# Sixteen gate units split by accumulating transfers, and a norm's two sums moved in TensorE's order

## The reference

```
h = x @ w_in + b_in
conv_a, conv_g, q, k, v, r, f_lr, gate_a, gate_b = split(h)
y_conv = conv_module(conv_a, conv_g, ...)      # 31 taps, layer norm over channels, silu, @ w_conv_out
y_gla  = gla_branch(q, k, v, r, f_lr, ...)     # gated linear attention, 4 chunks of 64, @ w_gla_out
merged = sigmoid(gate_a) * y_conv + sigmoid(gate_b) * y_gla
x = layer_norm(alpha * x + merged @ w_out + b_out)
x = layer_norm(alpha * x + hier_moe(x))        # 64 experts, 8 groups, top 2
```

## Time and profile before

| what | value |
|---|---|
| median of three runs | 1691.71 us |
| the profiled execution | 1691.89 us, of which the span is 1689.8 us |
| PE busy | 1364.6 us (81%) |
| DVE busy | 674.2 us (40%) |
| ACT busy | 472.0 us (28%) |
| POOL busy | 59.0 us (3%) |
| chain that ended last | PE 51%, DMA 39%, DVE 6%, ACT 3% |
| DMA | 530.79 MB, 314 GB/s over the span, 432 GB/s from 400 to 1180 us |

### The profile page before, as it was taken

One profiled execution on the slowest core, in us unless ns is written; L12 is line 12 of the kernel. 1 busy time (PEld: TensorE's weight loads), 2 busy tenths in 40 slices (PEclk: granted clock), 3 DMA queues, 4 the chain that ended last, 5 costly groups with the idle time before them and its releaser, 6 DMA issues.

```text
span 1689.8 us, 21326 instructions
## 1 busy us (share of the span) xinstructions
PE 1364.6 (81%) x8600; PEld 883.5 (52%) x8600; DVE 674.2 (40%) x1109; ACT 472.0 (28%) x682; POOL 59.0 (3%) x27
## 2 busy tenths in 40 slices
PE   8999999976656666665666667566799999999998
PEld 7789988522212212221221222122499999778887
DVE  5787979311101100110111011001367888655874
ACT  4454233401001001010010010010265764546653
POOL 0000000670000000000000000000000000000000
PEclk9999999988787978887888888788999999999999
DMA  9433555899999999999999999999944325474440
GB/s 359 156 138 138 218 204 245 353 431 430 432 431 431 431 433 433 431 431 432 433 433 431 431 432 433 431 432 431 419 165 150 139 71 197 167 258 175 179 174 25
DMA packets 50441, 530.79 MB, mean 314 GB/s; under 512 B 4276, under 2 KB 5556, under 8 KB 33862
## 3 DMA queue, kind: packets, MB, share of 16 engines
q1 hardware_dynamic: 50374, 529.86, 75.8%
HBM read 528.80 MB, written 1.05 MB: 314 GB/s over the span
## 4 chain that ended last, share of the span: by engine, by line
PE 51%; DMA 39%; DVE 6%; ACT 3%; issue 1%; SPq 0%; DVEq 0%; ACTq 0%
DMA shared<-in_w 37%; PE psum L454 6%; PE psum L456 6%; PE psum L455 6%; PE psum L1433 6%; PE psum L367 5%; PE psum L2222 4%; PE psum L1456 4%; PE psum L2223 2%; PE psum L1462 2%; PE psum L1404 2%; PE psum L2059 1%; DVE ring_parts L590 1%; DMA arena<-in_w 1%; PE psum L611 1%
## 5 line engine op out<-in xcount | busy, mean ns | idle before, releaser
L1433 PE MATMUL psum<-ring,arena 128*32 128x512 f32 x992 | 145.3, 739 | 86.8 <-DMA ring<-in_w 86.6
L1433 PE MATMUL psum<-shared,arena 128*32 128x512 f32 x1040 | 151.0, 726 | 61.5 <-DMA shared<-in_w 61.4
L1665 DVE TENSOR_TENSOR shared<-shared,psum 128x512 f32<-128x512 f32 x16 | 11.0, 688 | 462.3 <-PE psum L1433 462.3
L1456 PE MATMUL psum<-shared 128*32 128x512 f32 x512 | 89.5, 834 | 68.4 <-DMA shared<-in_w 68.4
L454 PE MATMUL psum<-parts 128*128 128x256 f32 (+1 forms) x424 | 136.5, 322 | 0.7 <-DVE parts L532 0.7
L455 PE MATMUL psum<-parts 128*128 128x256 f32 (+1 forms) x424 | 135.1, 319 | 0.0
L1433 PEld LDWEIGHTS psum<-ring,arena 128*32 128x32 f32 x992 | 34.3, 132 | 185.3 <-DMA ring<-in_w 100.2
L456 PE MATMUL psum<-parts,ring_parts 128*128 128x256 f32 x464 | 131.2, 283 | 0.0
L1433 PEld LDWEIGHTS psum<-shared,arena 128*32 128x32 f32 x1040 | 38.2, 129 | 168.3 <-issue 91.8
L456 PE MATMUL psum<-parts 128*128 128x256 f32 (+1 forms) x392 | 126.1, 322 | 0.0
L454 PE MATMUL psum<-parts,ring_parts 128*128 128x256 f32 x400 | 114.8, 287 | 0.4 <-ACT shared L2256 0.4
(11 more groups left out here) (343 smaller groups left out, 2347.4 us busy)
## 6 DMA issues: line engine op xcount, KB each, us to landing
shared<-in_w SPq DMA_DIRECT2D x47, 4096.0 KB, 32.4
ring<-in_w SPq DMA_DIRECT2D x47, 4096.0 KB, 32.4
ring<-in_w_in SPq DMA_DIRECT2D x19, 2048.0 KB, 8.7
ring<-in_w_ffn_gate_up SPq DMA_DIRECT2D x11, 2048.0 KB, 8.2
ring<-in_w_gate SPq DMA_DIRECT2D x8, 2048.0 KB, 7.9
ring<-in_w_ffn_down SPq DMA_DIRECT2D x5, 2048.0 KB, 7.8
ring<-in_w_out SPq DMA_DIRECT2D x4, 2048.0 KB, 8.6
shared<-in_w SPq DMA_DIRECT2D x6, 1024.0 KB, 28.8
```

The source lines that it names most:

```text
L1433: m = pe.matmul(ps[slots, bank, :], V.picked[:, k, slots], w[e * len(w) // QUAD][:, e % (QUAD // len(w)), j, :], start=(k == 0), stop=(k = ...
L1456: m = pe.matmul(ps[slots, MOE_BANK["down"][c], :], V.hidden_t[:, f, slots], w(e), start=(f == 0), stop=(f == ET - 1))
```

## The change

1. InSplit goes on through gb0 and gb1: units 44 to 51 are multiplied in three passes as well.
2. For units 36 to 51 (ga0 to gb1) the low half is not made by DVE. ACT writes the negated rounded weight into the low buffer (a first activation with scale -1), then the high, and GpSimd issues a DMA that reads the unit's weights again from HBM (w_in_units, 512 KB each) and adds them to the low buffer. PE waits for the high and for the landing of that DMA.
3. These units have four buffers (A-slots 6, 12, 13, 14). Slot 6 holds v until then, so ACT's step 36 waits for the last product with v (kv3_1).
4. The ring places of ga and gb are free once ACT has made the highs, no longer with the lows or the matmuls.
5. moe_read0 is raised after gb1.
6. DVE's loop has no lows from step 36 on; its pace there is 7 taps (4 at steps 39 and 40, where it was 1).
7. conv_mean stands after two tiles of go0 and conv_var after four, before half and three quarters; DVE's and go's order follow (EndSplit's first two lows come after the normalization).
8. Some semaphores are shared between stages (piece_in, router_exp); the loads of ga and gb are laid out by unit in HBM.

```diff
-    SLABS = ["g0", "a1", "g1", "k", "v0", "v1", "q", "r0", "r1", "ga0", "ga1"]
+    SLABS = ["g0", "a1", "g1", "k", "v0", "v1", "q", "r0", "r1", "ga0", "ga1", "gb0", "gb1"]
-    BUFS = 3
+    BUFS, WIDE = 3, 4
+    BY_DMA = 4 * SLABS.index("ga0")
...
+        slot = 12 + n % self.BUFS if n < self.BY_DMA else (6, 12, 13, 14)[(n - self.BY_DMA) % self.WIDE]
...
     def high(self, L, n):
         src = self.source(L.eng, n)
-        if n >= self.BUFS:
-            self.wait_read(L.eng, n - self.BUFS)
+        if n == self.BY_DMA:
+            self.K.banks1.wait_full(L.eng, f"kv{NC - 1}_1")
+        elif n >= self.BUFS:
+            self.wait_read(L.eng, self.before(n))
+        if n >= self.BY_DMA:
+            L.done(L.eng.activation(self.part(n, 1), src, ACT.Copy, scale=-1.0), self.K.sem("in_minus"))
         L.done(L.eng.activation(self.part(n, 0), src, ACT.Copy), self.K.sem("in_high"))
+
+    def low_by_dma(self, pool, n):
+        m = n - self.BY_DMA
+        pool.wait_ge(self.K.sem("in_minus"), m + 1)
+        pool.dma_start(self.part(n, 1).rearrange("p k n -> p (k n)"), self.K.d["w_in_units"][m], accum_op=ALU.add)\
+            .then_inc(self.K.sem(f"low_added{m % self.WIDE}"), 16)
...
     def wait_low(self, eng, n):
-        eng.wait_ge(self.K.sem("in_low"), n + 1)
+        m = n - self.BY_DMA
+        if m < 0:
+            eng.wait_ge(self.K.sem("in_low"), n + 1)
+        else:
+            eng.wait_ge(self.K.sem("in_high"), n + 1)
+            eng.wait_ge(self.K.sem(f"low_added{m % self.WIDE}"), 16 * (m // self.WIDE + 1))
...
     slab_tiles("ga1", "ga", 4)
+    for s in range(2):
+        slab_tiles(f"gb{s}", "gb", 4 * s)
     pe.drain().then_inc(S("moe_read0"), FREED)
-    for s in range(2):
-        pe_slab_tiles(K, pe, B, R, f"gb{s}", tiles("gb", 4 * s, 4), x)
     pe.wait_ge(S("gla_conv"), GLA_CONV["gla_in"])
     y = K.tiles(7, DT)
-    pe_slab_tiles(K, pe, B, R, "go0", tiles("go", 0, 4), y)
+    pe_slab_tiles(K, pe, B, R, "go0", tiles("go", 0, 2), y, last=False)
     pe.wait_ge(S("gla_conv"), GLA_CONV["conv_sum"])
     pe_group(K, pe, B, "conv_mean", ...)
-    pe_slab_tiles(K, pe, B, R, "go1", tiles("go", 4, 2), y, last=False)
+    pe_slab_tiles(K, pe, B, R, "go0", tiles("go", 2, 2), y, first=2)
     pe.wait_ge(S("conv_squares"), 1)
     pe_group(K, pe, B, "conv_var", ...)
-    pe_slab_tiles(K, pe, B, R, "go1", tiles("go", 6, 2), y, first=2)
+    pe_slab_tiles(K, pe, B, R, "go1", tiles("go", 4, 4), y)
...
-    for n in range(split.units):
-        split.low(L, n)
+    for n in range(split.BY_DMA + 8):
+        if n < split.BY_DMA:
+            split.low(L, n)
         done = n - split.BUFS
-        pace = 0 if done < 0 else 2 if done < 4 or 8 <= done < 12 else 4
+        pace = 0 if done < 0 else 2 if done < 4 or 8 <= done < 12 else 4 if n < split.BY_DMA else 7
...
-            pace = 1
+            pace = 4
...
-    for m in range(4):
+    for m in range(2):
         gate_gla(m)
-    lows(0, 2)
...
-    for m in (4, 5):
+    for m in (2, 3):
         gate_gla(m)
...
-    gate_gla(6)
+    lows(0, 2)
     for m in range(DT):
+        if m % 2 == 0 and m < 6:
+            gate_gla(4 + m // 2)
         act_parts(m)
...
+def block1_pool(K, pool):
+    split = InSplit(K)
+    for n in range(split.BY_DMA, split.units):
+        split.low_by_dma(pool, n)
```

More of the change, by code:

```diff
@@ L348, in rstd, with first_slab_at @@
         return self.A(2, T, 1024 if i == 3 else 240 + T * i)
+    def first_slab_at(self, slot):
+        return self.ring_cols(slot * SLOT_COLS, SLOT_COLS).rearrange("p (m k n) -> p m k n", m=4, k=DT)
     def first_slab(self, ring):
-        return self.ring_cols(ring.slot("a0") * SLOT_COLS, SLOT_COLS).rearrange("p (m k n) -> p m k n", m=4, k=DT)
+        return self.first_slab_at(ring.slot("a0"))
     def slab(self, slot, k=DT):
@@ L503, in part, with before @@
         k = 2 if self.SLABS[n // 4] in self.ROWS else DT
-        return self.K.parts(12 + n % self.BUFS, 1024, 1024 * low).rearrange("p (k n) -> p k n", k=k)
+        slot = 12 + n % self.BUFS if n < self.BY_DMA else (6, 12, 13, 14)[(n - self.BY_DMA) % self.WIDE]
+        return self.K.parts(slot, 1024, 1024 * low).rearrange("p (k n) -> p k n", k=k)
+    def before(self, n):
+        if n == self.BY_DMA:
+            return None
+        return n - (self.WIDE if n > self.BY_DMA else self.BUFS)
     def source(self, eng, n):
         slab, i = self.SLABS[n // 4], n % 4
-        w = self.K.slab(self.K.ring1.wait_landed(eng, slab))
+        slot = self.K.ring1.wait_landed(eng, slab)
+        if n >= self.BY_DMA:
+            return self.K.first_slab_at(slot)[:, i]
+        w = self.K.slab(slot)
         return w[:, 2 * i:2 * i + 2, :] if slab in self.ROWS else w[:, :, i * P:(i + 1) * P]
@@ L524, in high @@
         src = self.source(L.eng, n)
-        if n >= self.BUFS:
-            self.wait_read(L.eng, n - self.BUFS)
-        L.done(L.eng.activation(self.part(n, 0), src, ACT.Copy), self.K.sem("in_high"))
+        if n == self.BY_DMA:
+            self.K.banks1.wait_full(L.eng, f"kv{NC - 1}_1")
+        elif n >= self.BUFS:
+            self.wait_read(L.eng, self.before(n))
+        if n >= self.BY_DMA:
+            L.done(L.eng.activation(self.part(n, 1), src, ACT.Copy, scale=-1.0), self.K.sem("in_minus"))
+        L.done(L.eng.activation(self.part(n, 0), src, ACT.Copy), self.K.sem("in_high"))
+    def low_by_dma(self, pool, n):
[3 more added lines that the diff above has]
+            .then_inc(self.K.sem(f"low_added{m % self.WIDE}"), 16)
     def low(self, L, n):
@@ L535, in wait_low @@
     def wait_low(self, eng, n):
-        eng.wait_ge(self.K.sem("in_low"), n + 1)
+        m = n - self.BY_DMA
[4 more added lines that the diff above has]
+            eng.wait_ge(self.K.sem(f"low_added{m % self.WIDE}"), 16 * (m // self.WIDE + 1))
 class EndSplit:
     UNITS, CONV = 16, 8
-    READ, FIRST = 3 * len(InSplit.ROWS), 4 * len(InSplit.SLABS)
+    READ, FIRST, FIRST_LOW = 3 * len(InSplit.ROWS), 4 * len(InSplit.SLABS), InSplit.BY_DMA
     def __init__(self, K):
@@ L605, in block1_pe @@
     for m in range(4):
-        pe.wait_ge(S(f"first_in{m}"), 16)
+        pe.wait_ge(S(f"piece_in{m}"), 16)
         b = B.take(pe, f"a{m}")
@@ L736, in block1_pe @@
         b = B.take(pe, f"co{n}")
-        pe.wait_ge(S("in_low"), end.FIRST + n + 1)
+        pe.wait_ge(S("in_low"), end.FIRST_LOW + n + 1)
         w = end.part(n, 0), end.part(n, 1)
@@ L876, in outputs @@
             evac(f"ga{m}", K.tiles(8, DT)[:, m, :], ACT.Sigmoid, bias=K.v("b_ga", m))
+        elif slab in ("gb0", "gb1"):
+            m = i + 4 * int(slab[2])
+            evac(f"gb{m}", K.tiles(9, DT)[:, m, :], ACT.Sigmoid, bias=K.v("b_gb", m))
     kdec, o = K.tiles(10, TT, GDK, TT * GDK), K.tiles(4, DT)
@@ L904, in block1_act @@
                    B, "o_ms")
-    for m in range(DT):
-        evac(f"gb{m}", K.tiles(9, DT)[:, m, :], ACT.Sigmoid, bias=K.v("b_gb", m))
     end = EndSplit(K)
@@ L1221, in load_first @@
     def load_first(m):
-        sp.dma_start(first[:, m].rearrange("p k n -> p (k n)"), d["w_in_first"][m]).then_inc(S(f"first_in{m}"), 16)
+        sp.dma_start(first[:, m].rearrange("p k n -> p (k n)"), d["w_in_first"][m]).then_inc(S(f"piece_in{m}"), 16)
     def load_x(half):
@@ L1242, in load @@
         if before in InSplit.SLABS:
-            split.wait_low(sp, split.unit(before) + 3)
+            last = split.unit(before) + 3
+            if last < split.BY_DMA:
+                split.wait_low(sp, last)
+            else:
+                sp.wait_ge(S("in_high"), last + 1)
         elif before:
@@ L1475, in quad @@
         down(0, 2, lambda e: w1[:, 0, 0, e, :])
-        pe.wait_ge(S("w2_piece1"), n * 16 + 16)
+        pe.wait_ge(S("piece_in1"), n * 16 + 32)
         down(0, 3, lambda e: w1[:, 0, 1, e, :]).then_inc(S("down0"), 1)
-        pe.wait_ge(S("w2_piece2"), n * 16 + 16)
+        pe.wait_ge(S("piece_in2"), n * 16 + 32)
         down(1, 2, lambda e: w1[:, 1, 0, e, :])
@@ L1482, in quad @@
         put(0)
-        pe.wait_ge(S("w2_piece3"), n * 16 + 16)
+        pe.wait_ge(S("piece_in3"), n * 16 + 32)
         down(1, 3, lambda e: w1[:, 1, 1, e, :]).then_inc(ring.passed(i), 1)
@@ L1504, in moe_act @@
         L.done(act.activation(W.gexp[:, t, :], W.logits[:, t, 0:NG], ACT.Exp, bias=W.group_max[:, t:t + 1],
-                              accum_out=W.gsum[:, t:t + 1]), S("group_exp"))
+                              accum_out=W.gsum[:, t:t + 1]), S("router_exp"))
     act.wait_ge(S("expert_below"), 1)
     for t in range(TT):
-        L.done(act.activation(W.eexp[:, t, :], W.masked[:, t, :], ACT.Exp, bias=W.expert_max[:, t:t + 1]), S("expert_exp"))
+        L.done(act.activation(W.eexp[:, t, :], W.masked[:, t, :], ACT.Exp, bias=W.expert_max[:, t:t + 1]), S("router_exp"))
     for t in range(TT):
         L.done(act.activation(W.top2_exp[:, t, :], W.top8[:, t, 0:2], ACT.Exp, bias=W.expert_max[:, t:t + 1],
-                              accum_out=W.sums[:, t:t + 1]), S("expert_exp"))
```

(16 more changed lines are left out.)

## The result

The changed kernel is slower: 1699.47 us, the median of five runs (1697.82 to 1704.31), against 1691.72 us for before on the same chip (1690.87 to 1692.71). The ratio is 1.0052, with a 95% interval of 1.0041 to 1.0063. The profiled execution is the longest of the five, 1704.31 us.

The account below looks back on a forecast made before the run. The expert stage was taken as bound by its weight loads, the block before by PE, then PE and DVE. 1691.9 minus 8.65 gained plus 1.0 for late transfers gave 1684.2 us (1684.0 against the median), range 1681.5 to 1687.

Parts of the forecast that it names:

- gb's pitch: In gb, three passes take 2.88 us a tile instead of 3.45; eight tiles save 4.6 us on PE.
- the order: In go and co, earlier mean and variance spare PE the half-ready first co tile; 4.05 us gained.
- 8.65: Gain in us before moe_read3: 4.6 from gb and 4.05 from the earlier mean and variance.
- The last taps: DVE's taps before conv_mean end at 208.6 us, wanted at 213.8, so 5.2 us of cover.
- the moved load 0 or its queue: Load 0 waits for moe_read0 at 207 us, with co1, wo0, x_rows, wo1 behind it on SP; costs nothing.
- the price of the slab loads: In ga and gb, slab loads passing between the accumulating transfers make about seven units slightly late; 1.0 us for all.
- L: Time from the end of ACT's minus to PE's matmul, spent on an accumulating transfer; taken as 5.5 us.
- the bound of 6: Loss of about 6 us in ga and gb if transfers take their upper bound of 8.5 us.
- 7.0 allowed: In ga and gb, four buffers leave 7.0 us from the end of ACT's minus to the matmul.
- rival 2: In ga and gb, transfers set the pace without overlapping, 4.9 us a unit: 25 us lost, 1708; chance 0.22.
- rival 1: In ga and gb, transfers are partly late; at 8.0 us each, 5.5 us lost, time 1688.6; chance 0.15.
- Rival 3: The gain does not reach the end: load 0 and co1 in one queue, or stream start bound elsewhere; 1691; chance 0.08.

Follow-up runs that it names:

- co0 first: Changed kernel with co0, then go1 and the other slabs, loaded only after the last accumulating transfer has landed; 1685.90 us, ratio 0.9966.
- the old order: The late loads kernel with conv_mean and conv_var back after four and six tiles of go, DVE's order with them; 1689.61 us, ratio 0.9987.
- late loads: Changed kernel with go1, w_router, mem, a gain and co0 loaded only after the last accumulating transfer has landed; 1691.86 us, ratio 0.9993.
- one slab: Changed kernel with co0, mem and the gain waiting for the last accumulating transfer, go1 still loaded beside the transfers; 1691.66 us, ratio 0.9995.
- square first: The late loads kernel with ACT's first two highs of co placed behind the square; 1686.10 us, ratio 0.9963.

## Why the prediction was wrong

**What held.** gb's pitch fell to 2.88 us (ACT's readings of gb with co0 first: 203.39, 206.27, 209.14). The block gained 4.0 us by gb (the old order against before, with 0.6 us of a wait for a transfer in it), where 4.6 were forecast, and 4.0 by the order, where 4.05 were. Together 8.0 against 8.65. Of these 8.0 us in the block of co0 first, 6.5 are seen in the median. Other kernels lose more on the way: late loads has 3.8 us in the block and 0.5 in the median, one slab 3.0 and 0.7. Behind the first load after moe_read3 the two profiles of before take 1391.0 and 1390.8 us, co0 first 1390.8, late loads 1394.7, one slab 1394.0; what these 3 to 4 us are is open. The last taps ended at 211.7 us, 208.6 forecast plus, for the most part, the late start of 2.4. An add alone lands in 5.2 to 5.9 us, where 5.5 was taken. With co0 first PE has no wait from 120 to 260 us that the moved load 0 or its queue could have caused.

**The step that failed** is the price of the slab loads: "about seven units share the engines with one. For those L is 7.5 or so, each then 0.1 to 0.3 us late: I take 1.0 us for all". Measured are eleven units with landings of 8.0 to 13.4 us, and a cost of 162.8 - 146.9 = 15.9 us, beyond the bound of 6 too. Three things were wrong in it.

- The 7.5 is 2.0 us more than the 5.5 of an add alone, as if the engines had room for both; the prediction gives no working for it. The rate was checked in bytes, 182 GB/s beside a share of 0.36, and not in the engines' time. By the window of co0 first the adds fill the engines by themselves, so what a slab adds, 2 MB or about 4.9 us at 432 GB/s, is a backlog that all following adds carry: 5.5 + 4.9 = 10.4, and 9.9 to 10.9 were measured after go1 in one slab, 10.4 to 12.0 in the changed kernel. The 3.5 MB of mem, gain and co0 make 14.0 by the same sum and gave 12.7 to 13.4.
- The loss was taken as a few tenths for each unit. With L at 10 to 13 and 7.0 allowed it is one wait of 4.25 us and one of 6.28.
- The clock was named in rival 2 and left out of the sum. Each wait put the next tile at the lower level: 5.2 us instead of 2.88. Waits of 10.5 us and some 4.7 us of clock make up nearly all of the 15.9.

The time fell into the range of rival 2, at a chance of 0.22, but not by its mechanism: there one transfer ends before the next begins, and here landings of 10 us followed each other 2.7 us apart. The form is that of rival 1, transfers that land too late, with landings of 10 to 13 us where it reckoned with 8.0, and with the clock that rival 2 had named. Rival 3 is not what made the changed kernel slow; with co0 first and square first the greater part of the gain reaches the end.

The Trainium skill, in "Collectives: The Full Stack", section "The bandwidth ceiling", halves the rate of an add for its second source, and the trace agrees nearly: a share of 1.03 for the adds against 0.56 for copies of the same size at nearly the same rate. (The expert stage's 432 GB/s is no fair measure of it: its loads go in packets of 32 KB and these transfers in packets of 4 KB.) The Trainium skill, in "DMA: Bandwidth & Descriptors", section "Issuing engines are not separate DMA queues", says that transfers of GpSimd and SP run on the same 16 engines, and the trace agrees: GpSimd's adds landed after 10 to 13 us behind SP's loads, and after 5.2 to 5.7 with these loads moved. The prediction used the first for one transfer's time and not for the load of the engines.

## What to carry to other kernels

Before work is moved onto transfers, add up the engines' time in that stretch and not the bytes: an add held them 1.8 times as long as a copy here, and a stream that fills the engines turns each ordinary load into a delay for all that follows. Loads that are not wanted yet can then wait for the end of the stream; with co0 first among them, or the square ahead of its highs, that took the changed kernel from 0.5% slower to 0.3% to 0.4% faster, and without either only to the time of before. When a load is put back, look at what is queued behind its first reader, and when PE may wait for some us, count the lower clock behind the wait too.

## What was not expected of the hardware

A wait of 4 to 6 us cost TensorE about 2.3 us more by the clock, and ten to fourteen matmuls on constants in its place brought most of that back (0.50 to 1.00 in the granted clock). GpSimd's issue of an add takes 0.86 us, that of a copy of the same size 0.53. While DVE ran its taps without a break, adds landed as early as elsewhere (5.2 to 5.6 us from 180 to 200 us with co0 first). Two executions of the kernel before differ by 1.2 us at the first three-pass matmul (21.64 and 22.85 us; PE had waited 6.5 and 7.6 us for the load of x), and such a difference looks like an effect of the change if stages are read from the start of the span.
